# Strassen pairs in the last stage of a two-block transformer kernel: a pair's four summed products are issued on their own, behind the fifth weight piece after the pair's first

## The reference, cut to what matters

```
idx  = expert numbers of each token's top 16 of 8 heads      # out of 16384
gate = softmax(top_s)
act  = gelu(expert_u[idx] . h)
out  = sum_k gate * act * expert_v[idx]
```

## Time and profile before

| | us |
|---|---|
| median of 3 runs (lowest to highest) | 1460.01 (1459.71 to 1460.19) |
| the profiled execution's own time | 1459.59 |
| its span in the trace | 1457.8 |
| PE busy | 1419.6 (97% of the span) |
| PEld busy | 1271.6 (87%) |
| DVE busy | 1084.1 (74%) |
| ACT busy | 748.2 (51%) |
| POOL busy | 206.1 (14%) |

### The profile page before, as it was taken

How to read it: one execution, slowest core, us unless ns; L and a number is a source line. 1 busy time by engine, 2 the same in 40 slices (tenths; PEclk the granted TensorE clock), 3 DMA queues, 4 the chain that set the end, 5 groups by cost and what they waited for, 6 DMA issues and landing times.

```text
span 1457.8 us, 24725 instructions
## 1 busy us (share of the span) xinstructions
PE 1419.6 (97%) x10045; PEld 1271.6 (87%) x10045; DVE 1084.1 (74%) x2025; ACT 748.2 (51%) x1269; POOL 206.1 (14%) x101
## 2 busy tenths in 40 slices
PE   7999999999999889999999999999999999999998
PEld 6898797999888878979999999999998888888886
DVE  6677455665449897653898788999957888888886
ACT  5565453554336535344544555544445655655653
POOL 0037000000000020538685000000000000000000
PEclk9999999999999999999999999999999999999999
DMA  8634443555554510135566655555556666666663
GB/s 328 210 100 144 145 145 101 163 185 190 188 186 125 158 59 2 45 116 174 174 187 190 186 161 155 155 157 159 160 176 201 198 191 193 198 189 198 192 193 109
DMA packets 65617, 236.30 MB, mean 162 GB/s; under 512 B 7520, under 2 KB 7776, under 8 KB 65248
## 3 DMA queue, kind: packets, MB, share of 16 engines
q1 hardware_dynamic: 64784, 233.17, 51.0%
q10 hardware_dynamic: 720, 1.55, 0.3%
HBM read 233.65 MB, written 1.05 MB: 161 GB/s over the span
## 4 chain that ended last, share of the span: by engine, by line
PE 86%; DVE 9%; ACT 2%; issue 1%; DMA 0%; POOL 0%; DVEq 0%; ACTq 0%
PE ps L133 85%; DVE spl L158 2%; PE ps L142 1%; ACT spl L155 1%; DVE prep L158 1%; ACT QK L155 1%; DVE pm L167 1%; DVE pR L158 1%; DVE hx L158 0%; DVE pm L158 0%; DVE junk L158 0%; DMA hx<-in_xT 0%; DVE ez L167 0%; DVE qst L173 0%; ACT xhl L155 0%
## 5 line engine op out<-in xcount | busy, mean ns | idle before, releaser
L133 PE MATMUL ps<-xhl,spl 128*128 128x256 f32 x4944 | 606.3, 283 | 4.3 <-DVE spl L158 3.5
L133 PEld LDWEIGHTS ps<-xhl,spl 128*128 128x128 f32 x4944 | 591.2, 188 | 7.6 <-issue 6.4
L155 ACT ACTIVATE spl<-raw 128x1024 fp32r<-128x1024 f32 (+2 forms) x436 | 448.5, 1031 | 274.7 <-PE ps L133 265.7
L158 DVE TENSOR_TENSOR spl<-raw,spl 128x1024 fp32r<-128x1024 f32 (+2 forms) x371 | 440.9, 1194 | 194.0 <-ACT spl L155 188.3
L133 PE MATMUL ps<-spl,Wr 128*128 128x512 f32 x1266 | 300.8, 395 | 0.6 <-DVE Wr L158 0.5
L133 PEld LDWEIGHTS ps<-spl,Wr 128*128 128x128 f32 x1266 | 237.4, 188 | 59.0 <-DVE Wr L158 0.9
L158 POOL TENSOR_TENSOR spl<-raw,spl 128x1024 fp32r<-128x1024 f32 x65 | 165.4, 2556 | 83.6 <-ACT spl L155 83.2
L155 ACT ACTIVATE GE<-ps 128x256 f32<-128x256 f32 (+27 forms) x175 | 53.5, 322 | 108.2 <-DVE GE L167 108.0
L155 ACT ACTIVATE Wr<-GE 128x256 fp32r<-128x256 f32 (+1 forms) x128 | 49.6, 388 | 115.0 <-PE ps L133 115.0
L133 PE MATMUL ps<-spl,ahl 128*128 128x512 f32 x384 | 90.1, 396 | 0.0
L133 PEld LDWEIGHTS ps<-spl,ahl 128*128 128x128 f32 x384 | 72.2, 188 | 17.6
(11 more groups left out here) (362 smaller groups left out, 1345.5 us busy)
## 6 DMA issues: line engine op xcount, KB each, us to landing
raw<-in_eu SPq DMA_DIRECT2D x128, 512.0 KB, 3.6
raw<-in_ev SPq DMA_DIRECT2D x128, 512.0 KB, 3.6
raw<-in_w_up SPq DMA_DIRECT2D x32, 512.0 KB, 3.6
raw<-in_w_down SPq DMA_DIRECT2D x32, 512.0 KB, 4.3
raw<-in_w_in_a SPq DMA_DIRECT2D x16, 512.0 KB, 5.2
raw<-in_w_pq SPq DMA_DIRECT2D x16, 512.0 KB, 3.7
raw<-in_w_rwkv SPq DMA_DIRECT2D x14, 512.0 KB, 4.1
raw<-in_w_in_t SPq DMA_DIRECT2D x8, 512.0 KB, 3.5
```

Of the source, the lines that this page charges most:

```text
L133: return Done(self, self.e and self.e.matmul(out, l, r, start=st, stop=sp))
L155: return Done(self, self.e and self.e.activation(out, a, f, bias=bias, scale=scale, accum_out=acc))
L158: return Done(self, self.e and self.e.tensor_tensor(out, a, b, op))
```

## The change

`pair_mixed(s - 8)` is taken out of `pair_direct(s)`, and every pair's mixed products are now issued behind piece s+5, by the same rule for all. For the last pair this is one piece later than before. The number of matmuls, loads and vector instructions is the same.

```diff
@@ pair_direct(s)
                 pe.mm3(mixed[1][:, :], a11, (h1[:, 0:512], l1[:, 0:512]), s == PAIRS[0], s == PAIRS[-1]).then_inc("w_used", i1)
-                if s > PAIRS[0]:
-                    pair_mixed(s - 8)
                 pe.wait_ge(*low(i2))
                 pe.wait_ge("W", s + 1)
                 pe.mm3(bo[0, 0][:, :], a12, (h2[:, 0:512], l2[:, 0:512]), False, False)
@@ the loop over pieces on PE
                 elif not second(c):
                     apply((c,))
-                if c == PAIRS[-1] + 4:
-                    pair_mixed(PAIRS[-1])
+                if first(c - 5):
+                    pair_mixed(c - 5)
             apply((126, 127))
```

## The result

| | median of runs (lowest to highest), us | span of the profiled run, us |
|---|---|---|
| before, 4 runs | 1459.95 (1459.71 to 1460.19) | 1457.8 |
| changed, 4 runs | 1472.84 (1472.56 to 1473.26) | 1471.4 |

The ratio is 1.0089, with a 95% interval of 1.0076 to 1.0102: slower by 12.9 us. The forecast was 1473.7, in a range of 1471.5 to 1476.0.

The account below looks back on a forecast made before the run. The prediction took PE to bound the stage, with no idle time in its middle. It summed +15.1 us for 14 pairs and -1.4 us at the last pair to +13.7 us, 1473.7 us, range 1471.5 to 1476.0.

Parts of the forecast that it names:

- The bound: Whole stage: PE sets the time, 97% busy over the span, no idle middle; only waits can alter the time.
- 14 x 1.08 = 15.1 us for the pairs: At the 14 other pairs: each loses what pair 4 lost without mixed products inside, 1.08 us, together +15.1 us.
- the restart of 0.09 us: After pair 4's gap: the next 75 matmuls take 17.60 us where the pace gives 17.51.
- The waits of 0.35 and 0.64: At pair 4: 0.35 us lost before the third direct product (scores of piece 5), 0.64 us before piece 6.
- a chain of 2.95 us over a cover of 2.10 us: From piece 3's end to piece 6's start: refill takes some 2.95 us, 9 matmuls cover 2.10 us.
- Relief elsewhere does not shorten it: Refill at each pair: starts with piece s-1's end, so relief DVE and ACT get elsewhere leaves 1.08 us a pair.
- New place at nothing: Mixed products behind piece s+5: Tw is ready with 1.55 us to spare, so they cost nothing extra there.
- The last pair, -1.4 us: Pair 116: one piece later Tw is ready, so the 1.38 us lost there before comes back.
- only the 0.49 us in PE's row counts: At the pairs: the listed wait for DVE's Wr is the whole loss, +5.5, 1465.5 us; chance 0.05.
- The hidden refill: From piece s-1's end to scores of s+2: DVE and ACT run ahead, stalls go, 1458.6 us; chance 0.06.
- late Tw: Behind piece s+5: DVE's Tw is late at each of 15 places, 1.38 us each, 1494.4 us; chance 0.03.
- fall of the clock in the stage: After each pair's stall: 12 matmuls run at 1.2 GHz, adding 39 us, 1513 us; chance 0.02.

Follow-up runs that it names:

- runs 1 to 7: Seven follow-ups, mostly on the changed kernel, that moved the mixed products, altered piece s+2's split or exchanged direct products: from 1457.77 to 1475.25 us.
- Run 7: Changed kernel with second and third direct product exchanged: 1475.25 us; same exchange with mixed products directly behind the next pair: 1457.77 us.
- run 9: Changed kernel with the mixed products behind piece s+4 for every pair: 1495.61 us.
- Run 8: Kernel before with only the last pair's mixed products moved, behind piece 121 in place of 120: 1458.76 us.
- experiment 1: Changed kernel with the mixed products behind piece s+7, directly ahead of the next pair: 1458.42 us.
- experiments 3 and 8: The first: changed kernel with 3 of 12 mixed matmuls inside the next pair, the rest behind piece s+5: 1465.48 us; the other is Run 8.
- runs 8 and 10: The first is Run 8; the other: mixed products behind piece s+7, with piece 6 alone split in two halves: 1457.81 us.

## Why the prediction was right

By its own steps:

- **The bound.** PE with no idle time in the middle, so that only a new wait could count: it held. Matmuls, clock and pace (0.2335 us) are as before, and so nearly are the busy times of DVE (1082.3 us) and ACT (750.5 us), as forecast.
- **14 x 1.08 = 15.1 us for the pairs.** The mechanism is shown by runs 1 to 7; the size was 1.04, so 14.6 us. The term that was too large is the restart of 0.09 us, taken from pair 4: at pair 12 it is 0.04. The waits of 0.35 and 0.64 came as 0.34 and 0.66. One figure beside the sum does not fit it: a chain of 2.95 us over a cover of 2.10 us would lose 0.85 us, not the 0.99 that the rows of pair 4 show. The two were counted from different moments; from the start of the pair's first matmul the chain is 3.1 us. The sum went by the rows, so this did not touch it.
- **The wait for the scores and the wait for piece s+2.** The prediction listed them as two parts and then summed them as one chain. Run 7 shows that only the chain counts: the first part can be removed and the sum stays. Reading them as two separate savings would have been wrong.
- **"Relief elsewhere does not shorten it."** It held: ACT stood 1.54 us ahead of the chain at pair 12 in place of 1.20, and the chain took 2.85 us.
- **New place at nothing.** It held: no wait for Tw, and run 9 gives the margin, 1.39 us.
- **The last pair, -1.4 us.** Run 8 measures it alone: -1.43 us.
- **Sum.** +13.7 forecast; the stage shows 14.6 - 1.4 = 13.2, the medians 12.9. The difference between these two is well within the interval of the medians (11.1 to 14.9 us); what makes it lies ahead of the stage and between runs, and was not followed.

The rivals: that only the 0.49 us in PE's row counts would have given 1465.5; the loads' rows carry the other half. The hidden refill (1458.6) is excluded by the period of 22.754 us and the chain's unchanged 2.85 us. There was no late Tw, and no fall of the clock in the stage: the granted clock was 1.00 in both windows above and from 1110 to 1450 us, in spite of gaps every 22.75 us.

One thing is argued and not tried: which of the buffers holds the chain. The end of piece s-1 frees a split buffer and a Wr buffer at once, and ACT's scores of piece s+1, which wait for the Wr buffer, stand ahead of the refill in its queue. By that order a fourth split buffer alone would not start the chain earlier; no run has one.

## What to carry to other kernels

Work that seems to stand at an awkward place in an engine's order may be the cover of a refill: before moving it, find the event that frees the buffer, add up the chain from there to the next use, and count the work that stays in between. What counts is on which side of that event the work stands, not how close it is to its own kin: 12 matmuls directly ahead of the pair, but behind the event, did as well as inside it, and 6 inside were enough. Where a loop has a first or last round that lacks the work (here pair 4 and pair 116), its rows in the profile are a free experiment.

## What had not been expected of the hardware

In some executions the granted clock fell in a stretch of the program that no edit touches, over 460 us ahead of the stage. Windows of the profiled run of experiment 1 (columns as above):

```profile
600.00:620.00 20.00, 19.60 (x224) 18.59 (x220) 12.75 (x22) 5.21 (x10) 8.09 (x4) 0.90 0.19 53
620.00:640.00 20.00, 19.24 (x76) 15.54 (x77) 14.39 (x23) 8.02 (x13) 1.63 (x1) 0.85 0.31 89
640.00:660.00 20.00, 19.32 (x116) 15.77 (x115) 7.34 (x17) 10.92 (x18) 10.60 (x6) 1.00 0.41 123
```

The same stretch in the kernel before:

```profile
600.00:620.00 20.00, 18.27 (x237) 17.46 (x235) 13.80 (x25) 6.03 (x12) 7.73 (x4) 1.00 0.18 53
620.00:640.00 20.00, 19.70 (x88) 15.54 (x89) 15.40 (x24) 8.21 (x11) 3.16 (x3) 1.00 0.40 116
```

From 616 to 626 us the granted clock of experiment 1 reads 0.50, the level of 1.2 GHz; the 42 matmuls of 128x512 that start at 620.76 us take 12.49 us, where the same 42 take 10.05 in the kernel before. The profiled runs of experiments 3 and 8 show the same fall (0.91 and 0.83, 0.90 and 0.85 in the first two windows). Ahead of it PE does the same work in both: it is busy 1.61 of the 2 us from 614 to 616 us, and 1.63 in the kernel before, whose clock stays at 1.00. Nor is it a matter of the kernel: of the one before, 2 of 27 executions beside the first experiments took 1462.35 and 1462.38 us at a mean granted clock of 0.996. Why the clock falls in one execution and not in another was not tried. Two executions lie much further off and are not explained either: one of run 8 took 1546.21 us at a mean granted clock of 0.85, and one of 27 of the kernel before, beside runs 8 and 10, took 4295.71 us at 1.00.
